# Squares of the second GLA scan's finished chunks: from GpSimd to ScalarE, one step later

## The reference

```
y_l = out_fn(*lat_f, pre_lf) + jnp.flip(out_fn(*lb, pre_lb), axis=2)
...
y_gla = head_rms_norm(from_heads(o_gla, p.dtype), g_gla, N_GLA_HEADS) * jax.nn.silu(p[..., OFF_GLA_R:OFF_GLA_A])
return jnp.concatenate([y_ml, y_gla], axis=-1)
```

## Time and profile before

| | |
|---|---|
| median of 3 runs | 1386.4 us (1385.12 to 1390.82) |
| the profiled execution | 1388.91 us, of which its span is 1387.0 us |
| busy in the span | PE 92%, DVE 71%, ACT 54%, POOL 8% |
| the GLA scan | from about 576 to 645 us of the span |
| output projection | from 646.5 us to 757 us |
| squares and gate products on POOL | 8 of 1.04 us and 8 of 1.27 to 1.45 us, from 619.3 to 651.3 us |

### The profile page before, as it was taken

The page is one execution under the profiler, slowest core; times in us unless marked ns, Lnnn a source line. Parts: engine busy times, 40 slices in busy tenths (PEclk is TensorE's granted clock), DMA queues, the critical chain, the costliest instruction groups (busy, mean ns, idle before and its releaser), DMA issues.

```text
span 1387.0 us, 19391 instructions
## 1 busy us (share of the span) xinstructions
PE 1282.1 (92%) x7353; PEld 1119.9 (81%) x7353; DVE 977.9 (71%) x1223; ACT 753.0 (54%) x833; POOL 112.6 (8%) x114
## 2 busy tenths in 40 slices
PE   6899999899999999989999169999999999999994
PEld 5888799899987999867888158888888888888883
DVE  5858420399746673377544869888888888888887
ACT  7643310333412544574333337777777777777785
POOL 1100000000000000014000011111111111111034
PEclk9999989999999999999999569999999999999997
DMA  9840150001354322304112849999999999999995
GB/s 378 266 104 31 61 152 1 1 1 31 147 207 163 126 88 93 137 1 168 77 76 108 346 164 370 367 407 396 396 400 390 398 397 399 394 401 395 390 329 209
DMA packets 59901, 310.91 MB, mean 224 GB/s; under 512 B 5200, under 2 KB 13424, under 8 KB 30080
## 3 DMA queue, kind: packets, MB, share of 16 engines
q1 hardware_dynamic: 52640, 281.74, 51.3%
q0 software_dynamic: 7200, 28.31, 8.1%
HBM read 282.76 MB, written 35.67 MB: 230 GB/s over the span
## 4 chain that ended last, share of the span: by engine, by line
PE 75%; DVE 14%; ACT 5%; DMA 2%; issue 2%; SPq 0%; DVEq 0%; POOLq 0%; ACTq 0%
PE psum L2463 36%; PE psum L2128 6%; PE psum L2416 6%; PE psum L2186 5%; PE psum L2187 5%; PE psum L2188 5%; DMA ada_raw<-w_ada_units 1%; DVE ml_w L1527 1%; PE psum L2480 1%; PE psum L2029 1%; PE psum L2430 1%; DVE ml_c L1544 1%; PE psum L2486 1%; ACT g_ps L1075 1%; DVE left L1866 1%
## 5 line engine op out<-in xcount | busy, mean ns | idle before, releaser
L1896 DVE TENSOR_TENSOR e_lo<-e_raw,e_hi 128x2048 fp32r<-128x2048 f32 x192 | 432.9, 2289 | 45.9 <-ACT e_hi L1221 45.9
L1221 ACT ACTIVATE e_hi<-e_raw 128x2048 fp32r<-128x2048 f32 x192 | 365.9, 1917 | 88.1 <-PE psum L2463 87.5
L2463 PE MATMUL psum<-e_hi,xt_hi 128*128 128x512 f32 x496 | 154.4, 392 | 2.5 <-DVE xt_lo L1900 2.4
L2463 PE MATMUL psum<-e_lo,xt_hi 128*128 128x512 f32 x496 | 153.7, 391 | 0.0
L2463 PE MATMUL psum<-e_hi,xt_lo 128*128 128x512 f32 x496 | 153.7, 391 | 0.0
L2186 PE MATMUL psum<-w_hi,h_hi 128*128 128x256 f32 x512 | 148.3, 290 | 0.5 <-issue 0.5
L2187 PE MATMUL psum<-w_hi,h_lo 128*128 128x256 f32 x512 | 146.9, 287 | 0.0
L2188 PE MATMUL psum<-w_lo,h_hi 128*128 128x256 f32 x512 | 146.8, 287 | 0.0
L2463 PEld LDWEIGHTS psum<-e_hi,xt_hi 128*128 128x128 f32 x496 | 93.6, 189 | 22.8 <-DVE xt_lo L1900 3.4
L2463 PEld LDWEIGHTS psum<-e_hi,xt_lo 128*128 128x128 f32 x496 | 93.7, 189 | 19.7
L2463 PEld LDWEIGHTS psum<-e_lo,xt_hi 128*128 128x128 f32 x496 | 93.7, 189 | 19.7
(11 more groups left out here) (409 smaller groups left out, 2313.0 us busy)
## 6 DMA issues: line engine op xcount, KB each, us to landing
e_raw<-w_e_units SPq DMA_DIRECT2D x192, 1024.0 KB, 7.9
ada_x<-w_ada_units SPq DMA_DIRECT2D x16, 1024.0 KB, 4.8
raw<-w_in_units SPq DMA_DIRECT2D x14, 1024.0 KB, 6.3
ada_raw<-w_ada_units SPq DMA_DIRECT2D x8, 1024.0 KB, 21.8
xs<-x SPq DMA_DIRECT2D x4, 1024.0 KB, 10.3
acc_dram<-zero_r SPq DMA_DIRECT2D x1, 4096.0 KB, 17.9
wo_raw<-w_out SPq DMA_DIRECT2D x4, 1024.0 KB, 6.0
x_res<-xp_dram SPq DMA_DIRECT2D x4, 1024.0 KB, 6.6
```

Of the source, the lines that this page charges most:

```text
L1221: act.activation(e_hi[u % EH][:], e_raw[u][:], ACT.Copy).then_inc(e_hi_ok, 1)
L1896: dve.tensor_tensor(e_lo[u][:], e_raw[u][:], e_hi[u % EH][:], ALU.subtract).then_inc(e_lo_ok, 1)
L2463: m = pe.matmul(o[:, BANK * b:BANK * (b + 1)], x[:, k, :], w[:, D * j + BANK * b:D * j + BANK * (b + 1)], start=a, stop=z)
```

## The change

ScalarE makes the squares (`ACT.Square`, no accumulation), and GpSimd keeps the product with the gate, for which it now waits until the square is made (the product overwrites the tile). In ScalarE's loop the square of step `l-2` stands in step `l`, behind the exponentials and ahead of `gla_carry(l-1)`; those of the steps 14 and 15 stand behind the loop, around `yt_hi_part(0)`.

```diff
@@ GpSimd
             for l in range(TL, 2 * TL):
                 t = second_visit(l)
                 pool.wait_ge(og_done, l + 1)
-                if l >= TL + 2:
-                    pool.wait_ge(sq_read, l - TL - 1)
-                pool.tensor_tensor(g_sq[l % 2][:], og(t), og(t), ALU.mult).then_inc(gla_sq, 1)
+                pool.wait_ge(gla_sq, l - TL + 1)
                 v = og(t).rearrange("p (u n) -> p u n", u=2)
                 pool.tensor_tensor(v, v, silu_r(t), ALU.mult).then_inc(fin_done, 1)
@@ ScalarE
+            def gla_square(l):
+                act.wait_ge(og_done, l + 1)
+                if l >= TL + 2:
+                    act.wait_ge(sq_read, l - TL - 1)
+                act.activation(g_sq[l % 2][:], og(second_visit(l)), ACT.Square).then_inc(gla_sq, 1)
+
             gla_keys(0)
             for l in range(2 * TL):
                 if l + 1 < N_STATE:
                     gla_keys(l + 1)
                 if l + 2 < 2 * TL:
                     gla_exps(l + 2)
+                if l - 2 >= TL:
+                    gla_square(l - 2)
                 if 1 <= l <= N_STATE:
                     gla_carry(l - 1)
...
+            gla_square(2 * TL - 2)
             yt_hi_part(0)
+            gla_square(2 * TL - 1)
             yt_hi_part(1)
             head_sqrt(1)
```

## The result

The changed kernel takes 1394.51 us (median of 8 runs, 1392.10 to 1395.56), the kernel before in the same batch 1387.47 us (8 runs, 1385.12 to 1392.25): ratio 1.0045, 95% interval 1.0034 to 1.0057, so 4.7 to 7.9 us more. The time stands within the range of the prediction (1387.0 to 1395.0), 3.8 us above its figure and above the forecast's own range, which ended at 1393.

What follows compares the result with a forecast made beforehand. The scan's chain of waits, mostly on DVE, was taken to set the start of the PE-bound output projection. Carries 9 to 13 adding 1.34, 0.76 twice, 0.48 and 0.93 gave 1386.4 + 4.3 = 1390.7 us, range 1387.0 to 1395.0.

Steps and rivals of the forecast that it cites:

- The loop: Scan steps: ACT exponentials, square, DVE sums, addition, ACT carry, next keys in a row; 4.92 instead of 4.16 us, together +4.27.
- keys to last exponential: ACT's part of a scan step from the keys' copy to the last exponential's start: 1.15 us of the 4.92.
- The last term: Carry 12 to carry 13, with table load, root, square, sums and addition in a row: 5.09 instead of 4.16 us, +0.93.
- The clock: Rival, 15%: PE idles 2.7 us ahead of the output transposes, then runs at half speed, losing 1.7 to 3.5 us.
- the first rival: PE's clock falls after idling ahead of the output transposes, costing 1.7 to 3.5 us: 1392.4 to 1394.2 us; 15%.
- the rivals: Alternatives widening the range: PE's clock falls (15%), DVE is freed without new waits (6%), loss is absorbed behind 646 (8%).
- Freed DVE: Rival, 6%: in the scan the keys' product is no longer held, 1.1 us a step, and PE leads: 1385.2 us.
- The table load: Between carries 12 and 13: load taken as 1.30 us from the trace; the page's drain would make the whole +5.6.
- Absorbed: Rival, 8%: a wait behind 646 that does not shift takes up part of the loss: 1386.4 to 1388.5 us.

Runs made afterwards that it cites:

- e4: Changed kernel plus two matmuls whose result nobody reads, on TensorE ahead of its wait for the last carry; 1390.84 us, ratio 1.0018 to the kernel before.
- e1: Changed kernel with ScalarE's squares of steps 8 to 15 each made directly behind the carry of their own step; 1385.63 us, ratio 0.9982 to the kernel before.
- e5: Changed kernel with the loop's squares ahead of ScalarE's four exponentials instead of behind them; 1387.91 us, ratio 0.9995 to the kernel before.
- e3: Changed kernel with the five squares of steps 8 to 12 made twice on ScalarE, first copy unused; 1394.23 us, ratio 1.0046 to the kernel before.
- e7: Second run, in a later batch, of the changed kernel with the loop's five squares made twice; 1395.30 us, ratio 1.0051 to the kernel before.
- e8: The changed kernel itself, run again unaltered in a later batch; 1393.46 us, ratio 1.0040 to the kernel before.
- e2: Changed kernel with VectorE's sums of step l-2 behind the addition of step l-1 instead of ahead of it; 1387.05 us, ratio 0.9991 to the kernel before.
- e6: Changed kernel with the loop's five squares made twice and two unread matmuls ahead of TensorE's wait for the last carry; 1394.21 us, ratio 1.0050 to before.

## Why the prediction was nearly right

**The loop.** Its form was right in every link: sums waiting for the square, the addition behind them, the carry behind that. Measured 4.50 us against 4.27. By carries: 9, 5.34 us against 4.01 + 1.34 = 5.35; 10 and 11, 5.08 and 5.07 against 4.92; 12, 4.67 against 4.64; 13, 4.99 against 5.09. The mis-sized term is "keys to last exponential". I read the start of the first exponential from a step in which it stood 0.28 us behind the keys; in the changed steps it is 0.41 us (631.13 to 631.54), as it was in some steps of the kernel before (keys at 625.79, exponential at 626.20). Why the same pair overlaps in one step and not in another stays open. The square took 0.61 us against 0.62, DVE freed 0.46 us against 0.4 to 0.5. The last term was 0.10 us too long, since the square starts 0.22 us behind the root's start, and I had added the root's full 0.31.

**The clock.** The step that failed is the first rival's chance: the clock was given 15% and left out of the sum. Its mechanism, its place and its price stood in the text: PE idle for 2.7 us (measured 2.48), then 1.7 to 3.5 us lost (measured 1.66, just below its cheaper end; in all four profiles with that fall the pieces from the transposes to the projection take 6.05 or 6.06 us, so nothing shows the dearer one). It gave 1392.4 to 1394.2 us; measured were 1394.51 and 1393.46. I argued against it from a stretch in which PE's longest wait was 1.25 us, while the only row with a wait about as long as the one forecast, 3.02 us, showed a fall. e4 shows the cause: with the wait filled, 1.67 us go and nothing else in the stretch moves.

**The number.** The forecast's 4.27 us became 6.15 us in the stretch, 0.23 more in the loop and 1.66 for the clock. The time in the runs is 3.8 us above 1390.7 also because of its base: 1386.4 us was the median of 3 runs, and the 8 of the result's batch gave 1387.47, 1.07 us more. The rest of about 0.9 us is of the size of the runs' scatter. That the time lies inside the range at all is owed to the widening for the rivals, and the upper end, 1395.0, is only 0.5 us away.

**Freed DVE.** Rightly rejected for this order, and real: e1, where the square is ready in time, gains 1.34 us of the stretch (the text had 1.2, and TensorE in the lead), and 0.18% in the runs. The Trainium skill ("GPSIMD Engine Reference", "1. Specifications") says that GpSimd contends with VectorE where the instruction of VectorE has two SBUF inputs. The traces agree: the keys' product, which has two, takes 1.51, 1.06 or 0.46 us as it meets nearly the whole of POOL's product or less of it, and 0.42 us in e1, where it starts behind POOL's end, and the sums and the addition, which run beside it in the changed kernel, take their plain 0.69 us.

**The table load.** In the changed kernel the root starts 1.29 us behind the load's start (640.87, 642.16). No run here shows the drain of 1.38 us that the Trainium skill adds ("ScalarE: Activation LUTs", "What ACT_TABLE_LOAD costs"), and with it the loop's last term would have been 6.45 us instead of the 4.99 measured.

**Absorbed.** Nothing was, as far as the experts' start: 6.15 us at the projection are 6.24 us there, and about 6.0 us at the end of the profiled execution.

## What to carry to other kernels

When work moves from an idle engine to a busy one, ask first which instruction waits for it and what is queued behind that instruction; then look in the new engine's list for the last place that is still early enough. Here the same square gains 1.3 us right behind one carry (e1), comes out even one instruction later, behind the copy of the keys (e5), and loses 4.5 us in the loop, 6.15 with the clock, another four exponentials later. Then add the second-order cost: a longer wait of TensorE ahead of a stage in which it is full can cost a fall of its clock on top, and a few matmuls that nobody reads take that back. Take a term from the step that it stands in, not from one that looks alike.

## What the hardware showed

- In every profile in which PE had waited for 2.00 to 2.48 us ahead of the transposes (the changed kernel, e3, e7, e8), its clock was at 0.50 to 0.74 in the four whole microseconds behind their start and at 1.00 after those; where it had waited 1.53 us or less there (before, e1, e2, e4, e5, e6) it stayed at 1.00. A wait of 1.90 us in the loop was followed by a fall in e3 and e7 (1.90 and 1.91 us), and in e6 by none. The rows of e6, PE's timeline and the stretch behind it:

```profile
636.21 1.10 PE L2355 MATMUL psum<-gv,g_kt 128*128 128x256 f32 x4 [1.90 <-ACT g_ps L1073]
```

```profile
638.00:640.00 2.00, 1.91 (x12) 1.61 (x12) 1.56 (x3) 0.64 (x2) 1.27 (x1) 1.00 0.00 0
```

- The held product of the keys ends 0.27 to 0.29 us behind the end of POOL's instruction wherever it starts under it: before 629.42 against 629.14, after 635.03 against 634.75, in e2 628.34 against 628.05. Its plain time is 0.41 us, 0.13 more. DVE's `y_scale` (128x512, two SBUF inputs) gives the same picture: before, it took 0.91 us beside POOL's product and ended 0.55 us behind it (642.17 against 641.62), 0.14 less than its plain 0.69 us. So it looks like a wait for the end of POOL's instruction rather than a slower rate; no experiment was made on that alone.
